# A decoder step on one core: block 1's input rows taken between block 0's last value rows, with two routings beside them

## The reference

```python
def decoder_layer(x, past, g_attn, ...):
    mix, rows = token_mixers(rmsnorm(x, g_attn), past, w_in, ...)
    h = x + mix
    y = h + peer_ffn(rmsnorm(h, g_ffn), w_peer_q, peer_sub_keys, peer_u, peer_v)
    return y, rows

def one_block(xb):                       # 128 tokens
    q = jnp.einsum('td,de->te', xb, w_peer_q).reshape(PEER_BLOCK, PEER_HEADS, 2, PEER_DKEY // 2)
    s = jnp.einsum('thpc,hpkc->thpk', q, peer_sub_keys, preferred_element_type=jnp.float32)
    top_s, top_i = lax.top_k(s, PEER_TOPK)
    cand_s = ...                         # 16 x 16 sums and their expert numbers
    best_s, best_pos = lax.top_k(cand_s, PEER_TOPK)
    expert = jnp.take_along_axis(cand_i, best_pos, axis=-1)
    gate = jax.nn.softmax(best_s, axis=-1)
    u = peer_u[expert]
    act = jax.nn.gelu(jnp.einsum('thkd,td->thk', u, xb, ...), approximate=False)
    return jnp.einsum('thk,thkd->td', (gate * act).astype(peer_v.dtype), peer_v[expert])
```

## Time and profile before

| | us |
|---|---|
| median of 3 runs | 2368.76 |
| lowest, highest | 2368.74, 2373.32 |
| span of the profiled execution | 2358.0 |
| median less that span | 10.8 |
| PE busy in it | 1745.8 (74%) |
| DVE busy | 1134.5 (48%) |
| POOL busy | 1232.7 (52%) |
| ACT busy | 355.3 (15%) |
| moved by DMA | 784.77 MB, mean 333 GB/s |

### The profile page before, as it was taken

How to read it: one execution, slowest core, us unless ns; L and a number is a source line. 1 busy time by engine, 2 the same in 40 slices (tenths; PEclk the granted TensorE clock), 3 DMA queues, 4 the chain that set the end, 5 groups by cost and what they waited for, 6 DMA issues and landing times.

```text
span 2358.0 us, 32033 instructions
## 1 busy us (share of the span) xinstructions
PE 1745.8 (74%) x11231; PEld 710.9 (30%) x11231; DVE 1134.5 (48%) x2727; ACT 355.3 (15%) x761; POOL 1232.7 (52%) x1076
## 2 busy tenths in 40 slices
PE   8999849857777858789998888897566223337878
PEld 2555836522011433333333333331112000011212
DVE  1543888877503666645005676691000455551361
ACT  1222223301000113221112223221000000000000
POOL 0000236657767658836567886756333444564665
PEclk9999969979999879889999799999888555558999
DMA  5104548899999899999999999999999999999988
GB/s 219 27 23 181 194 148 278 293 412 330 345 369 358 307 318 399 399 323 377 399 400 366 368 399 397 398 386 366 403 401 401 408 404 404 404 384 355 349 308 316
DMA packets 258555, 784.77 MB, mean 333 GB/s; under 512 B 36593, under 2 KB 45450, under 8 KB 254938
## 3 DMA queue, kind: packets, MB, share of 16 engines
q0 software_dynamic: 150784, 547.43, 61.3%
q1 hardware_dynamic: 106442, 231.08, 26.4%
q10 hardware_dynamic: 1168, 4.23, 0.5%
HBM read 775.80 MB, written 6.81 MB: 332 GB/s over the span
## 4 chain that ended last, share of the span: by engine, by line
PE 40%; DMA 29%; SPq 9%; issue 7%; DVE 7%; POOL 5%; another core or an unknown queue 2%; ACT 1%; ACTq 0%; DVEq 0%; POOLq 0%
DMA arena<-peer_v,idxT 12%; DMA arena<-peer_u,eidx 10%; PE ps L1902 9%; PE ps L1964 7%; PE ps L1588 7%; POOL arena L552 5%; DMA arena<-vn_pool 4%; SPq L514 3%; DVE arena L1365 3%; SPq L511 3%; PE ps L1828 3%; DMA arena<-kpe_pool 2%; SPq L509 2%; PE ps L1950 2%; PE ps L1703 2%
## 5 line engine op out<-in xcount | busy, mean ns | idle before, releaser
L552 POOL DMA_INDIRECT arena<-peer_u,eidx x512 | 659.2, 1287 | 666.8 <-PE ps L1817 275.2
L1365 DVE CUSTOM_DVE_ANT_0 arena<-arena 128x1024 f32<-128x1024 f32 x512 | 619.6, 1224 | 697.3 <-DMA arena<-peer_u,eidx 672.8
L552 POOL DMA_INDIRECT arena<-peer_v,idxT x512 | 519.7, 1015 | 423.9 <-PE ps L1902 309.3
L1902 PE MATMUL ps<-arena 128*32 128x512 f32 x2048 | 554.5, 646 | 115.9 <-DMA arena<-peer_v,idxT 96.7
L1964 PE MATMUL ps<-arena 128*128 128x512 f32 x512 | 314.4, 700 | 45.7 <-DMA arena<-kpe_pool 43.3
L2034 PE MATMUL ps<-arena 128*32 128x512 f32 x512 | 104.6, 882 | 265.6 <-DMA arena<-vn_pool 264.1
L1902 PEld LDWEIGHTS ps<-arena 128*32 128x32 f32 x2048 | 105.1, 114 | 448.6 <-DMA arena<-peer_v,idxT 309.4
L879 ACT ACTIVATE arena<-ps 128x512 f32<-128x512 f32 x256 | 150.8, 596 | 462.1 <-PE ps L1964 273.9
L1588 PE MATMUL ps<-arena 128*128 128x512 f32 (+3 forms) x400 | 172.0, 584 | 0.4 <-DVE arena L1028 0.4
L1950 PE MATMUL ps<-arena 128*32 128x128 f32 x2048 | 148.2, 288 | 16.4 <-issue 8.7
L1964 PEld LDWEIGHTS ps<-arena 128*128 128x128 f32 x512 | 82.8, 202 | 106.6 <-issue 56.8
(11 more groups left out here) (310 smaller groups left out, 1566.8 us busy)
## 6 DMA issues: line engine op xcount, KB each, us to landing
arena<-kt_pool SPq DMA_DIRECT2D x256, 320.0 KB
arena<-vn_pool SPq DMA_DIRECT2D x256, 320.0 KB
arena<-w_q SPq DMA_DIRECT2D x16, 1024.0 KB, 13.7
arena<-w_in SPq DMA_DIRECT2D x8, 1236.0 KB, 15.7
arena<-w_o SPq DMA_DIRECT2D x16, 512.0 KB, 5.1
arena<-w_q SPq DMA_DIRECT2D x4, 2048.0 KB, 11.3
arena<-peer_u,eidx POOLq DMA_INDIRECT x512
arena<-peer_v,idxT POOLq DMA_INDIRECT x512
```

The costliest lines, as they stand in the source:

```text
L552: pool.indirect_dma_start(ring[:, q % RING, :], None, table, bass.IndirectOffsetOnAxis(ap=index, axis=0)).then_inc(g[q % RING], 16)
L1365: V_.tensor_tensor_reduce(rows, rows, x, 1.0, 0.0, ALU.mult, ALU.add, acc[:, k:k + 1]).then_inc(u_used, 1)
L1902: return T_.matmul(ps[32 * j:32 * j + 32, i, :], W32[:, j, c, :], ring[:, q % RING, 512 * i:512 * i + 512], start=(c == 0), stop=(c == 31) ...
```

## The change

Only the order of work changes. The order of gathers is now one list, `SEQ`, for all blocks: `LEAD[b]` value rows of block b, then block b+1's input rows and the rest of block b's value rows in turns. LEAD is [72, 128, 128], so blocks 1 and 2 go as before, and for block 0 it is 72 value rows, then u0, v72, u1, v73, ... u55, v127, and then u56 to u127 (u for block 1's input rows, v for block 0's value rows). `slot_free` makes each gather wait for the row eight places before it, whatever its kind.

On TensorE the 20 steps of route(2) and route(3) stand inside v_phase(0), at tokens 70, 73, 76, 79, 82, 84, 87, 90, 93, 96, 98, 101, 104, 107, 110, 112, 115, 118, 121 and 124; before each, the second half of the token before is brought forward. The `between` dictionary of u_phase(1) has its six pieces at dots 64, 68, 72, 76, 82 and 88. ScalarE stores block 0's result behind route_copies(3). Line numbers of the changed kernel differ by up to some 20 from those before (L552 is L557, L1902 is L1892).

```diff
@@ -57,6 +57,7 @@
 CW = PAST // NCH
 K_U1, K_V1, K_U2, K_V2 = range(0, 17), range(17, 32), range(32, 60), range(60, 64)
 S_U, S_V = 106, 119
+LEAD = [72, 128, 128]
 V_V2, V_U3 = range(0, 17), range(17, NPG)
 HPG = [4, 2, 1, 1]
 NG = [16 // m for m in HPG]
@@ -383,19 +384,23 @@
         def gcol(i):
             return 32 * (i % 4) + i // 4
 
-        LAST_ROWS = []
+        SEQ = [("u", 0, k) for k in range(P)]
+        for b in range(NB - 1):
+            SEQ += [("v", b, k) for k in range(LEAD[b])]
+            for k in range(P):
+                SEQ.append(("u", b + 1, k))
+                if LEAD[b] + k < P:
+                    SEQ.append(("v", b, LEAD[b] + k))
         for k in range(P):
             if S_U <= k < S_U + BD:
-                LAST_ROWS.append(("u", k - S_U))
+                SEQ.append(("su", SBLK, k - S_U))
             if S_V <= k < S_V + BD:
-                LAST_ROWS.append(("v", k - S_V))
-            LAST_ROWS.append(("token", k))
-
-        def row_of(kind, k):
-            return 2 * P * (NB - 1) + P + LAST_ROWS.index((kind, k))
-
-        def v_row(b, k):
-            return 2 * P * b + P + k if b < NB - 1 else row_of("token", k)
+                SEQ.append(("sv", SBLK, k - S_V))
+            SEQ.append(("v", NB - 1, k))
+        PLACE = {row: r for r, row in enumerate(SEQ)}
+
+        def row_of(kind, b, k):
+            return PLACE[kind, b, k]
 
 
         @block.sync
@@ -564,61 +569,46 @@
                                         bass.IndirectOffsetOnAxis(ap=lgi[:, i:i + 1], axis=0)
                                         ).then_inc(lg_gathered, 16)
 
-            for b in range(NB):
-
-                if b:
-                    pool.wait_ge(top_done, b + 1)
-                for k in range(SLOTS):
-                    if b == 0 and k % 32 == 0:
+            def index_ready(kind, b, k):
+                if kind == "u" and b == 0:
+                    if k % 32 == 0:
                         if k < 96:
                             pool.wait_ge(top_part, k // 32 + 1)
                         else:
                             pool.wait_ge(top_done, 1)
-                    if b == 2 and k % 2 == 0 and k < NPG:
-                        gather_logf((NPG + k) // 2)
-                    if b:
-                        pool.wait_ge(v_used, P * b + min(k - RING + 1, 0))
-                    if k >= RING:
-                        pool.wait_ge(u_used, P * b + k - RING + 1)
-                    gather(peer_u, eidx[:, k:k + 1], 2 * P * b + k)
-
-                if b == NB - 1:
-                    break
-                pool.wait_ge(idxT_done, b + 1)
-                for k in range(P):
-                    if b == 1 and k % 8 == 4:
-                        gather_logf(k // 8)
-                    if k >= RING:
-                        pool.wait_ge(v_used, P * b + k - RING + 1)
-                    else:
-                        pool.wait_ge(u_used, P * (b + 1) + k - RING + 1)
-                    gather(peer_v, idxT[:, gcol(k):gcol(k) + 1], 2 * P * b + P + k)
+                elif k == 0 and kind == "u":
+                    pool.wait_ge(top_done, b + 1)
+                elif k == 0 and kind in ("v", "su"):
+                    pool.wait_ge(idxT_done, b + 1)
 
             def slot_free(r):
                 if r < 0:
-                    pool.wait_ge(u_used, P * NB + r + 1)
                     return
-                kind, k = LAST_ROWS[r]
-                if kind == "token":
-                    pool.wait_ge(v_used, P * (NB - 1) + k + 1)
-                elif kind == "u":
+                kind, b, k = SEQ[r]
+                if kind == "u":
+                    pool.wait_ge(u_used, P * b + k + 1)
+                elif kind == "v":
+                    pool.wait_ge(v_used, P * b + k + 1)
+                elif kind == "su":
                     pool.wait_ge(s_u, k + 1)
                 elif k < BD - 1:
                     pool.wait_ge(s_v_used, k + 1)
                 else:
                     pool.wait_ge(s_v, 1)
 
-            pool.wait_ge(idxT_done, NB)
-            for r, (kind, k) in enumerate(LAST_ROWS):
+            for r, (kind, b, k) in enumerate(SEQ):
+                index_ready(kind, b, k)
+                if kind == "v" and b == 1 and k % 8 == 4:
+                    gather_logf(k // 8)
+                if kind == "u" and b == 2 and k % 2 == 0 and k < NPG:
+                    gather_logf((NPG + k) // 2)
                 slot_free(r - RING)
-                if kind == "token":
-                    gather(peer_v, idxT[:, gcol(k):gcol(k) + 1], row_of(kind, k))
-                elif kind == "u":
-                    if k == 0:
-                        pool.wait_ge(idxT_done, NB + 1)
-                    gather(peer_u, idxS[:, k:k + 1], row_of(kind, k))
+                if kind == "u":
+                    gather(peer_u, eidx[:, k:k + 1], r)
+                elif kind == "v":
+                    gather(peer_v, idxT[:, gcol(k):gcol(k) + 1], r)
                 else:
-                    gather(peer_v, idxS[:, k:k + 1], row_of(kind, k))
+                    gather(peer_u if kind == "su" else peer_v, idxS[:, k:k + 1], r)
 
 
         @block.scalar
@@ -905,8 +895,8 @@
             load_h(0)
             gate_exp(1)
             route_copies(2)
+            route_copies(3)
             store_y(0)
-            route_copies(3)
 
             act.wait_ge(dq_done, 1)
             act.wait_ge(d_ps, 1)
@@ -1358,7 +1348,7 @@
                 for k in range(lo, hi):
                     for f in between.get(k, []):
                         f()
-                    q = 2 * P * b + k
+                    q = row_of("u", b, k)
                     dve.wait_ge(g[q % RING], 16 * (q // RING + 1))
                     rows = heads(ring[:, q % RING, :], P, 2)
                     x = heads(xn2[:, b, :], P, 2)
@@ -1493,8 +1483,8 @@
             top_subkeys_of(1)
             top_experts(1)
             open_gates(1)
-            u_phase(1, {8: [lambda: add_y(0)], 30: [lambda: copy_idxT(1)], 38: [lambda: finish_gates(1)],
-                        54: [decode_queries_1], 60: [decode_queries_2], 66: [log_gate_rows]})
+            u_phase(1, {64: [lambda: add_y(0)], 68: [lambda: copy_idxT(1)], 72: [lambda: finish_gates(1)],
+                        76: [decode_queries_1], 82: [decode_queries_2], 88: [log_gate_rows]})
             combine_chunk(0)
             top_subkeys_of(2)
             top_experts(2)
@@ -1547,7 +1537,7 @@
             copy_idxT(SBLK)
             V_.tensor_copy(dsm[:, 56:64], ps[:, 7, 8:16]).then_inc(s_gT, 1)
             for k in range(BD):
-                q = row_of("u", k)
+                q = row_of("su", SBLK, k)
                 dve.wait_ge(g[q % RING], 16 * (q // RING + 1))
                 dve.wait_ge(s_xb, k + 1)
                 V_.tensor_tensor_reduce(heads(ring[:, q % RING, :], P, 2), heads(ring[:, q % RING, :], P, 2),
@@ -1897,7 +1887,7 @@
                 if b:
                     pe.wait_ge(y_done, b)
                 def half(k, i):
-                    q = v_row(b, k)
+                    q = row_of("v", b, k)
                     c, j = k // 4, k % 4
                     return T_.matmul(ps[32 * j:32 * j + 32, i, :], W32[:, j, c, :],
                                      ring[:, q % RING, 512 * i:512 * i + 512], start=(c == 0), stop=(c == 31),
@@ -2052,20 +2042,12 @@
                 if k == P - 1:
                     end_unit(units[-1])
 
-            def route(b):
-                turn_rows(b)
-                query_rows(b, 0)
-                query_rows(b, 1)
-                turn_queries(b, 0)
-                query_rows(b, 2)
-                turn_queries(b, 1)
-                subkey_scores(b, 0)
-                query_rows(b, 3)
-                turn_queries(b, 2)
-                subkey_scores(b, 1)
-                turn_queries(b, 3)
-                subkey_scores(b, 2)
-                subkey_scores(b, 3)
+            def route_steps(b):
+                return [lambda: turn_rows(b), lambda: query_rows(b, 0), lambda: query_rows(b, 1),
+                        lambda: turn_queries(b, 0), lambda: query_rows(b, 2),
+                        lambda: (turn_queries(b, 1), subkey_scores(b, 0)), lambda: query_rows(b, 3),
+                        lambda: (turn_queries(b, 2), subkey_scores(b, 1)), lambda: turn_queries(b, 3),
+                        lambda: (subkey_scores(b, 2), subkey_scores(b, 3))]
 
             def late_scores(k):
                 i, o = k // 8, k % 8
@@ -2074,12 +2056,12 @@
                 if k == 8 * len(K_V2):
                     end_unit(K_V2[-1])
 
-            route(1)
+            for f in route_steps(1):
+                f()
             turn_w(0)
-            v_phase(0)
-            route(2)
+            steps = route_steps(2) + route_steps(3)
+            v_phase(0, {70 + 3 * i - i // 5: f for i, f in enumerate(steps)})
             turn_idx(1)
-            route(3)
             turn_decode_queries()
             absorb_decode_queries()
```

(2 more changed lines are left out.)

## The result

The changed kernel takes 2401.8 us (median of 4 runs) against 2371.04 for the kernel before, run beside it: ratio 1.0138, 95% interval 1.0094 to 1.0181. It is slower by 1.4%, where 2363.5 and "faster" were forecast, and outside the range of 2352 to 2382. "Slower" was the side of rival B.

A forecast was written before the change was run, and what follows sets the result against it. DMA engines bound most of the span, idle 16 us from 790 to 869. S 9.5 us later, S to T 14.7 shorter, T 5.2 earlier: span 2352.8, plus 10.8 around it, forecast 2363.5, range 2352 to 2382.

The forecast's parts named there:

- rival B: Alternating gathers of blocks 0 and 1: the eight-slot ring binds behind long routing steps; 12 us later than forecast, 2375.5; chance 0.24.
- The row order to X: Alternating u and v gathers, 52 at 1.28 us and 51 at 1.425, then landing and last routing step: X at 810.2, 31 us earlier.
- X: SP's request for the decode constants, when route 3's last copy is done: 841.69 us before, forecast 810.2.
- The routes between tokens: Routing steps on TensorE among block 0's tokens: two long steps without a short one between, twice, charged 3 us.
- T: Start of block 1's values: 1029.78 us before, forecast 1024.6, 5.2 us earlier.
- S: Start of K_U1 on TensorE: 868.66 us before, forecast 878.2, 9.5 us later.
- The dots ahead of K_U1: Decode queries move to dots 76 and 82, so K_U1 starts behind 82 dots, not 60; S 9.5 us later.
- K_U1: The decode keys' scores, 17 units on TensorE ahead of block 1's values; S to T forecast 14.7 us shorter.
- A: Alternating gathers run freer than charged, at 398 GB/s, 1.317 us a row: T 9 us earlier than forecast, 2354.5; chance 0.22.
- C: The tail of K_U1 doesn't speed up, units take 8 us: T 4.5 us later than forecast, 2368; chance 0.09.
- D: Dots hold GpSimd's gather issue in the alternating stretch, 1.97 us instead of 0.94: 54 us, 2417; chance 0.03.
- A shift of T is a shift of the end: Behind block 1's values all queues keep their order, so the end moves by as much as T, 5.2 us earlier.

The follow-up runs named there:

- both repairs: Changed kernel with query blocks cut in steps of 4 matmuls, one after every second token, and decode queries at dots 58 and 64: 0.9983 of the kernel before, 0.9974 repeated.
- prompt release: Changed kernel with both halves of each block 0 token from 70 on run back to back, so its slot is given back at once: ratio 1.0152 to the kernel before.
- second group: Runs on one chip: kernel before repeated 1.000, changed kernel 1.0187, changed kernel with early decode queries 1.0035, that with query blocks cut in two as well 0.9983.
- two-to-one version: Changed kernel with query blocks cut in two, one u row after every two v rows, and block 1's side work from dot 32: ratio 0.9940 to the kernel before.

## Why the prediction was wrong

**The row order to X: the step that failed.** The working had v123 139.2 us behind u0 and charged 3 us for the routes, 142.2 together; the trace has 168.8, 26.5 us more. u0 itself came 2.1 us later, and from v123 to X it took 11.9 us, where landing and last step (5.9 + 3) had been put at 8.9. So X came 31.6 us later than forecast. Two causes of the 26.5, the first shown by the experiments, the second by the share beside the pace:
- *The routes between tokens.* I charged 3 us on an average: TensorE has less work than there is time. The four profiles of the changed kernel have 167.1 us from u0 to v123, the three profiles with both repairs and full dots 153.4 (one of them with the prompt release too). So the long steps cost 13.7 us in the means (10.4 in the pair of one group, 167.0 against 156.6). In T they cost 12.8 in each of two pairs; but in the first of these the version with long steps had the prompt release as well, and in the second 5.3 arose behind S, where the step has no known part. Rival B had this mechanism; it gave 15 us where the upper bound was 45, and the measured cost lies by its 15. What misled me was the sum of TensorE's work against the time of the rows. The sum itself was right, as the two-to-one version shows (125 us), but not what I took from it. As I read the rows, with eight slots in two streams only some four v rows lie between a stop of TensorE and a stop of the gathers, and what is lost then isn't caught up: the DMA engines, at a share of 0.97 to 0.98 in the versions without long steps, have no slack to catch up with.
- *The price of a u row.* I took 1.28 us from eight gathers and 1.425 for a v row. With the routings away, a mixed row took 1.43 at 0.98 share. Eight gathers in a stretch whose share was 0.80 weren't a rate that the DMA engines hold.
The account from u0 to v123: 103 mixed rows at 1.43 us take 147.3, 8.1 more than the 139.2 worked out; the three versions with both repairs take 6.1 more than that, for which I have no single cause (they spread from 149.7 to 156.6); long steps 13.7 more again; and the profile shown lies 1.7 above the mean of its four.

**The dots ahead of K_U1.** X to S was forecast at 68.0 and took 67.2; S to T 146.4 and 144.0. Here the mechanism was right too. From X to dot 75 the DMA engines moved 398 GB/s (the row 842 to 890 above), 19.2 MB where 19.5 were reckoned. The tail ran at TensorE's own pace: the last five units took 7.1 us each but for the very last, 7.74, and GpSimd's wait was 56.56 us where some 55 were forecast. What the late queries cost shows in the second group: with X as it was, early ones bring T 14.5 us forward. That is one pair of profiles, as are the 12.8 of the long steps. By the means the two together are worth 33.4 us (T 1053.8 against 1022.5, 1018.0 and 1020.7): the 24.3 by which T is late, and 9.1 by which it is ahead of the kernel before without them. In the time these three versions are at 0.9971 to 0.9983, and only one of the three intervals leaves 1 out.

**The rivals.** A (gathers run freer) is refuted: the mixed row isn't cheaper. B was right in its place and price (T 12 later than forecast), but not by itself: T came 28 us later than forecast, some 14 of it from B and the rest from the price of a row, the 6.1 us without a single cause, the step behind v123 and the start. B alone would have given 2375.5. C: the tail's units took 7.1 to 7.7 us, no part. D (dots hold the gathers' issue): the mechanism is there, 12.3 us in the 31 issues over 1.0 us of the stretch instead of 54 us in 52. On the version with both repairs halving the dots removed four fifths of it and gained nothing in pace.

**"A shift of T is a shift of the end".** Not refuted and not shown: over four profiles of each, T to the end differs by 13 us with an interval that holds zero. Of the 30.8 us between the two medians, 24.3 lie ahead of T; where the rest arises stays open. A kernel's own spread behind T is 20 to 30 us from run to run, more than all that was forecast, and the working knew nothing of it. The same spread was in the base: I took 10.8 us between the span and the median as what lies around the span. In the later runs the time of a profiled execution is 1.8 above its span; the other 9 lie between the profiled execution and the timed ones.

## What to carry to other kernels

When two consumers share a ring, price an insertion by its longest single piece against the slots that its stream has in the ring, and not only by the sum of the work against the time: the same routings in pieces of 3.7 us, dealt out evenly, cost some 14 us less than in pieces of 7.1. A rate read from a handful of rows in a stretch that waits for something is not the transfer's rate; take it where the DMA share is near one. And where work is moved forward, first look at what its follower stands behind: here the mix that filled both TensorE's time in the alternating stretch and the DMA engines' in the tail won 0.6%, while the even mix with long steps and late decode queries lost 1.4%.

## What was not expected of the hardware

A gather's issue on GpSimd is held by a dot that is already under way, and not by one that begins after it. GpSimd's and VectorE's timelines of the version with both repairs (second group):

```profile
688.32 1.97 POOL L557 DMA_INDIRECT arena<-peer_u,eidx  x1 [0.30 <-issue]
690.60 0.94 POOL L557 DMA_INDIRECT arena<-peer_v,idxT  x1 [0.30 <-issue]
691.84 1.91 POOL L557 DMA_INDIRECT arena<-peer_u,eidx  x1 [0.30 <-issue]
694.05 0.94 POOL L557 DMA_INDIRECT arena<-peer_v,idxT  x1 [0.30 <-issue]
```

```profile
688.26 1.22 DVE L1355 CUSTOM_DVE_ANT_0 arena<-arena 128x1024 f32<-128x1024 f32 x1 [6.43 <-DMA arena<-peer_u,eidx]
...
691.71 1.23 DVE L1355 CUSTOM_DVE_ANT_0 arena<-arena 128x1024 f32<-128x1024 f32 x1 [2.22 <-DMA arena<-peer_u,eidx]
...
694.33 1.23 DVE L1355 CUSTOM_DVE_ANT_0 arena<-arena 128x1024 f32<-128x1024 f32 x1 [1.38 <-DMA arena<-peer_u,eidx]
```

The dots end at 689.48 and 692.94, the held issues at 690.29 and 693.75, 0.81 us later both times; the issue at 694.05 began 0.28 us ahead of a dot and took its usual 0.94. In the changed kernel's alternating stretch no issue that began outside a dot took over 0.94 us (71 of them), and the 30 that began in one with over 0.2 us to go ended 0.80 to 0.82 us behind it. With half dots the longest issue took 1.44 us.

The 54 dots of that stretch of the changed kernel took 1.22 to 1.23 us, whether an issue was under way or not. In other profiles a few dots that began within 0.04 us of an issue took a little longer, up to 1.30 us (702.32 in the two-to-one version), and the issue beside them took its usual 0.94. The Trainium skill (SBUF — State Buffer, "Who interferes with whom") has a VectorE instruction with two SBUF inputs contend with GpSimd instructions that read SBUF, and the order of issue decide who waits. The traces bear out the first. The second they bear out for the gather, which waits for a dot that began well ahead of it; a dot beside an issue lost 0.07 us at most.
